# Attention weights multiplied on GpSimd instead of VectorE, in a two-block transformer kernel

## The reference

```python
sc = einsum('bgrqd,bgkd->bgrqk', qb, kwb) * scale
pw = masked_softmax(sc, okw)
o_win = einsum('bgrqk,bgkd->bgrqd', pw, vwb)
out = g[..., 0:1] * o_cmp + g[..., 1:2] * o_slc + g[..., 2:3] * o_win
```

## Time and profile before

| | us |
|---|---|
| median of 3 executions | 889.99 (889.47 to 891.58) |
| the profiled execution | 889.47 |
| its span, first to last instruction | 887.7 |
| TensorE matmuls busy in the span | 857.1 (97%) |
| VectorE busy | 551.0 (62%) |
| ACT busy | 456.3 (51%) |
| GpSimd busy | 37.3 (4%) |

### The profile page before, as it was taken

How to read it: one execution, slowest core, us unless ns; L and a number is a source line. 1 busy time by engine, 2 the same in 40 slices (tenths; PEclk the granted TensorE clock), 3 DMA queues, 4 the chain that set the end, 5 groups by cost and what they waited for, 6 DMA issues and landing times.

```text
span 887.7 us, 13979 instructions
## 1 busy us (share of the span) xinstructions
PE 857.1 (97%) x5975; PEld 784.9 (88%) x5975; DVE 551.0 (62%) x687; ACT 456.3 (51%) x667; POOL 37.3 (4%) x44
## 2 busy tenths in 40 slices
PE   5999999999999999999999999999989999999995
PEld 5899998889799999899999999878868899999994
DVE  4672486667766767577766776665775654554444
ACT  4463467777665634455554554535654443443441
POOL 0100200000000000100000000012110000000001
PEclk9999999999999999999999999999999999999998
DMA  6545524232243377265455455375325455555521
GB/s 251 184 144 219 174 83 139 76 135 80 88 175 135 122 251 276 96 225 202 155 185 209 164 190 190 142 261 190 100 82 216 179 185 192 187 190 190 190 95 47
DMA packets 22077, 146.40 MB, mean 165 GB/s; under 512 B 2432, under 2 KB 2688, under 8 KB 7552
## 3 DMA queue, kind: packets, MB, share of 16 engines
q1 hardware_dynamic: 20880, 140.27, 44.2%
q10 hardware_dynamic: 1136, 5.24, 1.6%
HBM read 144.45 MB, written 1.05 MB: 164 GB/s over the span
## 4 chain that ended last, share of the span: by engine, by line
PE 87%; DVE 5%; ACT 4%; issue 2%; DMA 1%; POOL 1%; SPq 0%; DVEq 0%; POOLq 0%; ACTq 0%
PE PS L1402 17%; PE PS L1404 17%; PE PS L1403 17%; PE PS L1413 9%; PE PS L1414 9%; PE PS L1415 9%; PE PS L1638 3%; PE PS L1439 1%; PE PS L1495 1%; PE PS L1472 1%; PE PS L1621 1%; ACT WH L540 1%; PE PS L1443 1%; PE PS L1390 1%; DVE WL L875 1%
## 5 line engine op out<-in xcount | busy, mean ns | idle before, releaser
L875 DVE TENSOR_TENSOR WL<-RAW,WH 128x2048 fp32r<-128x2048 f32 (+3 forms) x130 | 288.5, 2222 | 137.6 <-ACT WH L540 137.4
L540 ACT ACTIVATE WH<-RAW 128x2048 fp32r<-128x2048 f32 (+3 forms) x130 | 241.0, 1855 | 106.0 <-PE PS L1415 54.3
L1402 PE MATMUL PS<-BH,WH 128*128 128x256 f32 (+2 forms) x776 | 220.6, 284 | 0.2 <-DVE BL L882 0.2
L1404 PE MATMUL PS<-BH,WL 128*128 128x256 f32 (+2 forms) x776 | 219.6, 283 | 0.0
L1403 PE MATMUL PS<-BL,WH 128*128 128x256 f32 (+2 forms) x776 | 219.6, 283 | 0.0
L1402 PEld LDWEIGHTS PS<-BH,WH 128*128 128x128 f32 (+2 forms) x776 | 145.5, 188 | 2.4 <-issue 1.7
L1403 PEld LDWEIGHTS PS<-BL,WH 128*128 128x128 f32 (+2 forms) x776 | 145.4, 187 | 0.4
L1404 PEld LDWEIGHTS PS<-BH,WL 128*128 128x128 f32 (+2 forms) x776 | 145.7, 188 | 0.0
L1402 PE MATMUL PS<-CH,WH 128*128 128x256 f32 x448 | 126.8, 283 | 0.2 <-DVE CL L882 0.2
L1403 PE MATMUL PS<-CL,WH 128*128 128x256 f32 x448 | 126.8, 283 | 0.0
L1404 PE MATMUL PS<-CH,WL 128*128 128x256 f32 x448 | 126.8, 283 | 0.0
(11 more groups left out here) (251 smaller groups left out, 1143.4 us busy)
## 6 DMA issues: line engine op xcount, KB each, us to landing
RAW<-in_w_stream SPq DMA_DIRECT2D x109, 1024.0 KB, 4.8
RAW<-in_w_stream SPq DMA_DIRECT2D x12, 896.0 KB, 4.7
RAW<-in_w_stream SPq DMA_DIRECT2D x8, 768.0 KB, 4.3
WF<-in_w_stream SPq DMA_DIRECT2D x4, 784.0 KB, 4.8
WF<-in_w_stream SPq DMA_DIRECT2D x2, 1024.0 KB, 4.8
LN<-in_ln ACTq DMA_DIRECT2D x2, 1024.0 KB, 5.2
X<-in_x SPq DMA_DIRECT2D x2, 512.0 KB, 3.8
X<-in_x ACTq DMA_DIRECT2D x1, 1024.0 KB, 6.1
```

The costliest lines, as they stand in the source:

```text
L540: eng.activation(WH[:, c % NSLOT, 0:CHUNKS[c][2]], raw(c), ACT.Copy).then_inc(w_hi, 1)
L875: eng.tensor_tensor(WL[:, c % NSLOT, 0:CHUNKS[c][2]], raw(c), f32(WH[:, c % NSLOT, 0:CHUNKS[c][2]]), ALU.subtract).then_inc(w_lo, 1)
L1402: eng.matmul(out, wh, H[0:parts, k, :], start=(k == 0), stop=False)
L1404: last = eng.matmul(out, wl, H[0:parts, k, :], start=False, stop=(k == nk - 1))
```

## The change

The multiply of SM by wt moves from VectorE to GpSimd, for all 16 units. GpSimd gets a loop over the units in its queue, behind `kc_rstd`; it waits for wt of the unit and signals `p_ready`, for which the transposes wait. VectorE no longer waits for its own wt. Because GpSimd now reads wt while VectorE may go on, VectorE waits, before it writes wt of unit u, until P of unit u-2, which used the same buffer, is done.

```diff
@@ gpsimd, behind the power of kc_rstd
+            for u in range(NU):
+                qt = (u >> 1) & 1
+                eng.wait_ge(wt_ready, u + 1)
+                s = sm_view(SM, u, qt)
+                w = heads4(wt, 4 * (u % 2)).unsqueeze(3).broadcast_to([P, 2, 2, P * (qt + 1)])
+                eng.tensor_tensor(s, s, w, ALU.mult).then_inc(p_ready, 1)
@@ vector, unit_weights(u)
                 gate = gts[:, 48 * qt + 12 * g + br + 1:48 * qt + 12 * g + br + 11:3]
+                if u >= 2:
+                    eng.wait_ge(p_ready, u - 1)
                 eng.tensor_tensor(wt[:, o:o + 4], ri_[:, o:o + 4], gate, ALU.mult).then_inc(wt_ready, 1)
-                eng.wait_ge(wt_ready, u + 1)
-                s = sm_view(SM, u, qt)
-                w = heads4(wt, o).unsqueeze(3).broadcast_to([P, 2, 2, P * (qt + 1)])
-                eng.tensor_tensor(s, s, w, ALU.mult).then_inc(p_ready, 1)
```

## The result

The changed kernel takes 900.24 us (median of 4 executions, 899.24 to 902.27) against 889.73 before: ratio 1.0113, 95% interval 1.0092 to 1.0136, 10.5 us slower. The forecast was 896.6 in a range of 889.3 to 902, with 0.80 on slower. The sign and the range held; the sum of +7.1 us was 3.4 us short of the 10.5, and the time lies above the forecast's own range of 893 to 899.5. The profiled execution took 899.83 us.

What follows compares the result with a forecast made beforehand. The prediction took TensorE to bound the kernel (87% of the chain); late multiplies at some units, less 0.68 us gained at scores 7, summed to +7.1 us, giving 896.6 us in a range of 889.3 to 902.

Steps and rivals of the forecast that it cites:

- the time saved on VectorE is worth next to nothing: Units 0 to 15: 15.4 us of multiplies leave VectorE, nearly all of it hidden behind TensorE.
- WL shuts GpSimd out: Behind wt, WL starts first where WH is ready; GpSimd waits 2.20 or 1.94 us before its multiply can finish.
- nothing gives the loss back later: Behind 262 us the chain is TensorE again, so the +7.1 us stays.
- rival A: All units: GpSimd starts 0.08 us behind wt, undisturbed by VectorE; about +0.1, 889.5 us; chance 0.15.
- Rival B: Scores 7 and 13 come earlier by 0.68 and 1.15 us, GpSimd being undisturbed and quick: 887.7 us; chance 0.05.
- GpSimd takes its turn behind XC: Units 5 and 11: GpSimd gets in after XC, ahead of WL; -0.68 and +1.10 us.
- rival C: Units 5 and 11: VectorE keeps its turn, GpSimd waits for XC and WL; +4.1, 900.7 us; chance 0.13.
- rival D: Units 3, 7, 15: TensorE's clock falls in the longer waits, costing up to 4.5 us: 901.1 us; chance 0.12.
- The large multiply: GpSimd's multiply for a large unit, taken as twice the 1.29 us RQK add: 2.58 us, bounds 1.0 and 3.15.
- Units 3, 7 and 15: Large units whose multiply ends after WL, delaying TensorE's transposes: +2.08, +1.48 and +2.17 us.
- Units 6, 9 and 13: Units where GpSimd's multiply behind WL makes the transposes slightly late: +0.30, +0.32 and +0.30 us.
- the three signs by which the forecast called itself wrong: GpSimd's times independent of VectorE, large multiply alone far from 2.6 us, or clock leaving 1.00 between 126 and 270 us.

Runs made afterwards that it cites:

- The first experiment: The changed kernel, all 16 multiplies on GpSimd, but VectorE's WL there waits until P is ready: 889.68 us, ratio 0.9994 to the kernel before.
- XC first: The kernel before, nothing on GpSimd, with XC ahead of the reciprocal, wt and multiply at units 5 and 11: 888.18 us, ratio 0.9984.
- the probe: Two runs of the kernel before plus work on unused tiles, timing GpSimd operations alone and beside rows of VectorE instructions; total time says nothing.
- the spare matmuls: The changed kernel with 10 and 18 unread matmuls on TensorE ahead of the transposes of units 5 and 11: 895.24 us, ratio 1.0072.

## Why the prediction was right, and where it was off

Right: that the time saved on VectorE is worth next to nothing, that WL shuts GpSimd out and its multiply ends behind WL, which units suffer and which don't (2, 4, 8, 10 and 14 cost nothing, as said) but for unit 5, and that nothing gives the loss back later. The first experiment settles rival A, no shutting out: where WL waits, the loss is gone. Rival B, the gain through the VectorE stretches, did not occur; it exists (scores 7 came 0.7 us early where WL waits, and 1.0 with XC first), but needs P in time.

Off, in three steps:

"GpSimd takes its turn behind XC", at units 5 and 11. It did not; rival C, given 0.13, happened: +2.27 instead of -0.68 and +3.71 instead of +1.10 with the clock in it, +0.95 and +2.45 without it, where C had +1.2 and +3.3. I had taken the boundary between two 128-partition instructions at 368 us for the rule. XC covers 112 partitions and WL 128. By the probe GpSimd misses such a boundary; whether the step up in partitions does it or a long instruction behind a narrow one is not shown, and the reason is open.

The clock, rival D, priced at units 3, 7 and 15 with up to 4.5 us. There the waits were 0.6 to 1.3 us and the clock stayed. It fell behind the two long waits that rival C made: from the transposes to the next scores 2.95 instead of 1.63 us, and 3.77 instead of 2.55, with the tail 2.8 us. C and D were priced apart, but the waits behind which the clock fell were C's. The argument against D, that the clock stayed at 1.00 behind a wait of 1.63 us, was weak: with all units but 5 and 11 on GpSimd it fell behind that very wait.

The large multiply, taken as 2.58 us: 1.90. Units 3, 7 and 15 add 0.64 us less each for it. Units 6, 9 and 13 add 0.1 to 0.2 less (unit 6's 0.22 is the clock; with the spare matmuls it adds nothing); at the small ones, 9 and 13, the multiply ends 0.90 us behind WL, where 1.15 was counted. In all that is 2.4 us less than forecast. Estimating from the Trainium skill (GPSIMD Engine Reference, "Performance versus the Vector engine"), 2.2 us, was nearer; the probe's 2.24 us for 976 elements is close to its figure, and only the spread factor is cheaper.

The errors partly cancelled: +5.6 us at units 5 and 11, -2.4 at the others. That the time fell into the range is in part luck: the range was wide enough to take in C and D, and 900.24 is nearer to C's 900.7 than to the forecast. Two of the three signs by which the forecast called itself wrong came up, a large multiply alone far from 2.6 us (1.90) and a granted clock that left 1.00; the third, GpSimd's times not depending on VectorE, did not.

## What to carry to other kernels

Before work moves from VectorE to GpSimd, look at what VectorE does next: if that has two SBUF operands, the moved instruction ran behind it here, and the delay to count is nearly both durations (3.88 us for 1.90 beside a WL of 2.28). If the moved result is urgent and the next VectorE instruction is not, make the latter wait for it. A move of urgent work is better answered by order on the same engine: putting the two instructions that others wait for ahead of those nobody waits for yet gave 0.4% (1.8 us of it seen in the traces) where the move cost 1.1%.

## What the runs showed of the hardware

- A GpSimd tensor_tensor waiting beside VectorE instructions with two SBUF operands got in behind the first of them (1.62 us for a 128x512 multiply beside 768 columns), except where that one covered 96 or 112 partitions and the next covered 128 with 2032 columns or more: then it got in behind the second (3.81 us). 112x768 followed by 112x768, and 128x768 followed by 112x2032, let it in. Whether the partitions or the length of the next decides was not tried.
- VectorE pays too: a 112x1 instruction lasted 1.00 us and AL 2.65 instead of 0.95, behind a multiply of GpSimd's. The Trainium skill (SBUF — State Buffer, "Who interferes with whom") says that the one that issues first keeps the other out; the runs agree, but for the exception above.
- A GpSimd multiply with a factor repeated along the row takes 1.04 us for 128x512 and 1.90 for 128x1024; with two full operands 1.27 for 512 and 2.24 for 976.
- Behind two waits of TensorE, of 2.4 and 4.2 us, its clock fell from 2.4 to 1.2 GHz for some 3 us each; filled with spare matmuls they left it at 1.00. Shorter waits went either way: behind 1.95 to 2.09 us at unit 11 it fell in three traces, behind 1.63 us at unit 7 it fell in one (0.52) and stayed at 1.00 in the kernel before.
